# Attention's value products with the values stationary, two heads on the two column halves

## The reference

```python
def causal_block_attention(q, k, v):
    B, S, H, Dq = q.shape
    nb = S // Q_BLOCK
    scale = Dq ** -0.5
    qb = q.reshape(B, nb, Q_BLOCK, H, Dq).transpose(1, 0, 2, 3, 4)
    kpos = jnp.arange(S)

    def one_block(args):
        qi, idx = args
        s = jnp.einsum('blhd,bshd->bhls', qi, k, preferred_element_type=jnp.float32) * scale
        qpos = idx * Q_BLOCK + jnp.arange(Q_BLOCK)
        s = jnp.where(kpos[None, :] <= qpos[:, None], s, -jnp.inf)
        p = jax.nn.softmax(s, axis=-1).astype(v.dtype)
        return jnp.einsum('bhls,bshd->blhd', p, v)
...
    q = (rms_norm(c_q, q_gain) @ w_uq).reshape(B, S, A_HEADS, A_QK_DIM)
    kv = (rms_norm(c_kv, kv_gain) @ w_ukv).reshape(B, S, A_HEADS, A_NOPE + A_V_DIM)
...
    o = causal_block_attention(q, k, v)
```

## Time and profile before

| | |
|---|---|
| median of 3 runs | 1856.79 us |
| lowest, highest | 1854.67, 1859.2 us |
| span of the profiled execution | 1858.9 us |
| PE busy | 1745.5 us (94%) |
| DVE, ACT, POOL busy | 733.7, 424.0, 345.4 us |
| mean granted clock of TensorE | 0.974 |

### The profile page before, as it was taken

How to read it: one execution, slowest core, us unless ns; L and a number is a source line. 1 busy time by engine, 2 the same in 40 slices (tenths; PEclk the granted TensorE clock), 3 DMA queues, 4 the chain that set the end, 5 groups by cost and what they waited for, 6 DMA issues and landing times.

```text
span 1858.9 us, 25203 instructions
## 1 busy us (share of the span) xinstructions
PE 1745.5 (94%) x9534; PEld 1034.3 (56%) x9534; DVE 733.7 (39%) x1955; ACT 424.0 (23%) x1143; POOL 345.4 (19%) x381
## 2 busy tenths in 40 slices
PE   9999998888899999989799887999999999999998
PEld 5566555544446556655554443645668555466764
DVE  1844526421113462534721111334565233356533
ACT  3433321011112332322011111121332112123221
POOL 1100320332221010131133221000242000014300
PEclk9999989998999999989899998999999999999999
DMA  6121035899998111007599999612033121201401
GB/s 243 39 95 46 1 159 226 341 422 416 377 385 348 57 68 71 40 1 294 217 370 381 383 392 397 250 58 78 35 82 120 37 102 46 91 35 47 154 2 45
DMA packets 72535, 322.88 MB, mean 174 GB/s; under 512 B 26348, under 2 KB 40236, under 8 KB 50912
## 3 DMA queue, kind: packets, MB, share of 16 engines
q1 hardware_dynamic: 61536, 304.46, 41.8%
q0 software_dynamic: 10880, 16.82, 2.6%
HBM read 401.68 MB, written 28.85 MB: 232 GB/s over the span
## 4 chain that ended last, share of the span: by engine, by line
PE 80%; DMA 9%; DVE 6%; issue 3%; ACT 2%; SPq 1%; POOL 0%; POOLq 0%; DVEq 0%; ACTq 0%
PE bank L642 16%; PE bank L2444 10%; PE bank L1022 10%; PE bank L2430 8%; DMA b_arena<-in_w 7%; PE bank L1042 5%; PE bank L654 4%; PE bank L2619 3%; PE bank L2610 3%; PE bank L626 3%; PE bank L1007 1%; PE bank L2413 1%; PE bank L729 1%; PE bank L716 1%; PE bank L2405 1%
## 5 line engine op out<-in xcount | busy, mean ns | idle before, releaser
L642 PE MATMUL bank<-b_arena 128*128 128x512 f32 (+2 forms) x768 | 311.4, 558 | 5.3 <-DMA b_arena<-in_w_a 2.2
L1022 PE MATMUL bank<-b_arena,b_nat 128*32 128x256 f32 (+1 forms) x3008 | 258.7, 394 | 45.9 <-issue 27.9
L1022 PEld LDWEIGHTS bank<-b_arena,b_nat 128*32 128x32 f32 (+1 forms) x3008 | 156.5, 126 | 167.8 <-issue 80.4
L2444 PE MATMUL bank<-b_actT,b_ring 128*128 128x512 f32 x512 | 224.0, 594 | 0.0
L642 PEld LDWEIGHTS bank<-b_arena 128*128 128x128 f32 x768 | 144.5, 194 | 136.0 <-issue 105.1
L1500 DVE TENSOR_TENSOR b_nat<-bank,b_prm 128x512 f32<-128x512 f32 x68 | 47.0, 692 | 360.4 <-PE bank L1001 332.2
L2430 PE MATMUL bank<-b_ring,b_actT 128*128 128x384 f32 (+1 forms) x512 | 171.8, 492 | 3.0 <-DVE b_actT L3331 2.1
L2444 PEld LDWEIGHTS bank<-b_actT,b_ring 128*128 128x128 f32 x512 | 96.0, 190 | 114.9 <-issue 113.8
L1042 PE MATMUL bank<-b_arena,b_ebuf 128*32 128x512 f32 (+1 forms) x752 | 131.4, 601 | 19.1 <-ACT b_ebuf L1349 17.0
L2430 PEld LDWEIGHTS bank<-b_ring,b_actT 128*128 128x128 f32 x512 | 95.7, 190 | 70.4 <-issue 22.7
L1472 POOL DMA_INDIRECT y_rows<-b_va,b_rows_ix x68 | 69.6, 1023 | 343.5 <-ACT b_va L1357 334.7
(11 more groups left out here) (395 smaller groups left out, 2292.7 us busy)
## 6 DMA issues: line engine op xcount, KB each, us to landing
b_arena<-in_w SPq DMA_DIRECT2D x94, 2048.0 KB
b_arena<-in_w SPq DMA_DIRECT2D x94, 1024.0 KB
b_ring<-in_w_t SPq DMA_DIRECT2D x8, 2048.0 KB, 8.0
b_arena<-in_w SPq DMA_DIRECT2D x8, 1536.0 KB, 10.8
b_ring<-in_w_n2b SPq DMA_DIRECT2D x6, 1536.0 KB, 7.3
b_arena<-in_w_out SPq DMA_DIRECT2D x4, 2048.0 KB, 7.7
b_arena<-y_rows SPq DMA_DIRECT2D x16, 512.0 KB, 7.7
b_ring<-in_w_out SPq DMA_DIRECT2D x4, 2048.0 KB, 11.3
```

The source lines that it names most:

```text
L642: ins = pe.matmul(bank[:, 0:width], actT[:, k, tok(i)], w[:, k, :], start=k == 0, stop=k == KD - 1)
L1022: ins = pe.matmul(psum[2 + b % 2][f * CAP + at:f * CAP + end, 0:256], xgT[:, b % 2, k % 4, k // 4, at:end], w[half][:, k, f, :], start=k = ...
L2444: ins = pe.matmul(bank[:, :], w[:, k, tok(u % 4)], actT[:, k, :], start=k == 0, stop=k == KD - 1)
```

## The change

The roles of the operands are exchanged: the values (128x64) are loaded as the stationary operand and the transposed exponentials (128x128) stream past. The result is transposed: 64 value columns on partitions and 128 queries in the columns. Head 2p goes to partitions 0 to 63 and head 2p+1 to 64 to 127 of the same bank region. Since the rest of the kernel wants the queries on the partitions, ScalarE copies the result to SBUF (`oT`, in `w_uq`, which is free by then), PE transposes it back into a new bank (`on`, the same helper as for the exponentials), and VectorE copies it to `nat` as before. The work comes in ten groups a layer (`VALUES_AT`): tile 0 whole at u = 3; the pairs of heads of tile 1 at u = 4, 5, 6; those of tile 2 at 8, 10, 12; those of tile 3 at 14, 16, 18. `turn_values(g)` stands at the head of the next `attend`, the last one behind `out(0, 0)`. Twenty uses of banks take the place of 17, so most later uses have another bank and another predecessor than before. `a_squares` and `a_sums` of tiles 0, 1 and 2 move behind the next `attend`.

```diff
+VALUES_AT = [(3, 0, (0, 1, 2)), (4, 1, (0,)), (5, 1, (1,)), (6, 1, (2,))]
+VALUES_AT += [(8 + 6 * (i - 2) + 2 * p, i, (p,)) for i in (2, 3) for p in range(3)]
...
-        return [("sc", u)] * (u < UNITS) + [("pT", u - 1)] * (1 <= u <= UNITS) + [("av", u - 2)] * (u >= 2)
+        return ([("on", GROUP_AT.get(u - 1))] * (u - 1 in GROUP_AT) + [("sc", u)] * (u < UNITS)
+                + [("pT", u - 1)] * (1 <= u <= UNITS) + [("av", GROUP_AT.get(u))] * (u in GROUP_AT))
...
+            def turn_values(l, g):
+
+                _, _, ps = VALUES_AT[g]
+                pe.wait_ge(*emptied(l, "av", g))
+                transposed(l, "on", g, len(ps), lambda n: oT[:, g % 2, tok(n)])
+
             def attend(l, u):
 
+                if u - 1 in GROUP_AT:
+                    turn_values(l, GROUP_AT[u - 1])
...
-                if u >= 2:
-                    i, hs = UNIT[u - 2]
-                    pe.wait_ge(*emptied(l, "pT", u - 2))
-                    pe.wait_ge(*vacant(l, "av", u - 2))
-                    bank, full = writer(l, "av", u - 2)
-                    for n, h in enumerate(hs):
+                if u in GROUP_AT:
+                    g = GROUP_AT[u]
+                    _, i, ps = VALUES_AT[g]
+                    for t in sorted({unit_of(i, 2 * p + a) for p in ps for a in range(2)}):
+                        pe.wait_ge(*emptied(l, "pT", t))
+                    pe.wait_ge(*vacant(l, "av", g))
+                    bank, full = writer(l, "av", g)
+                    for n, p in enumerate(ps):
                         for j in range(i + 1):
-                            ins = pe.matmul(bank[:, n * AV:(n + 1) * AV], probT[:, u % 2, tok(n * (i + 1) + j)],
-                                            va[:, j, h, :], start=j == 0, stop=j == i)
+                            for a in range(2):
+                                t = unit_of(i, 2 * p + a)
+                                at = (2 * p + a - UNIT[t][1][0]) * (i + 1) + j
+                                ins = pe.matmul(bank[a * AV:(a + 1) * AV, tok(n)], va[:, j, 2 * p + a, :],
+                                                probT[:, t % 2, tok(at)], start=j == 0, stop=j == i)
...
                 out(l, 0, 0)
+                turn_values(l, VALUES - 1)
...
                     if u >= 3:
-                        act.wait_ge(*filled(l, "av", u - 3))
+                        act.wait_ge(*filled(l, "av", GROUP_OF[u - 3]))
                     copy_out(l, "pT", probT[:, (u - 1) % 2, 0:len(hs) * (i + 1) * P], u - 1)
+                if u in GROUP_AT:
+                    g = GROUP_AT[u]
+                    if g >= 2:
+                        act.wait_ge(*filled(l, "on", g - 2))
+                    copy_out(l, "av", oT[:, g % 2, 0:len(VALUES_AT[g][2]) * P], g)
...
-                attend(l, 18)
                 halves(l, "yT", 0, PC["mix"])
+                values_out(l, VALUES - 1)
```

More of the change, by code:

```diff
@@ L33, with unit_of @@
 UNITS = len(UNIT)
+VALUES_AT = [(3, 0, (0, 1, 2)), (4, 1, (0,)), (5, 1, (1,)), (6, 1, (2,))]
+VALUES_AT += [(8 + 6 * (i - 2) + 2 * p, i, (p,)) for i in (2, 3) for p in range(3)]
+VALUES = len(VALUES_AT)
+GROUP_AT = {v: g for g, (v, _, _) in enumerate(VALUES_AT)}
+def unit_of(i, h):
+    return next(u for u, (tile, hs) in enumerate(UNIT) if tile == i and h in hs)
+GROUP_OF = [next(g for g, (_, tile, pairs) in enumerate(VALUES_AT) if tile == i and hs[0] // 2 in pairs)
+            for i, hs in UNIT]
+assert all(VALUES_AT[GROUP_OF[u]][0] <= u + 3 for u in range(UNITS))
 M_AT = [0, S, 2 * S - P, 3 * S - 3 * P]
@@ L224, in order_one @@
     use += attend(14) + [("c", 2), ("csg", 0)] + attend(15) + [("csg", 1), ("c", 3)] + attend(16) + attend(17)
-    use += pair("yT", 0) + attend(18) + [("wo", 0), ("csg", 2), ("wo", 1)] + pair("yT", 1) + [("csg", 3), ("wo", 2)]
+    use += pair("yT", 0) + attend(18) + [("wo", 0), ("on", VALUES - 1), ("csg", 2), ("wo", 1)] + pair("yT", 1) + [("csg", 3), ("wo", 2)]
     use += pair("yT", 2) + [("wo", 3)] + pair("fT", 0) + [("wo", 4)] + pair("fT", 1) + [("route", 0)] + pair("yT", 3)
@@ L432, in block_one @@
         nat_flat = nat[:, :, :].rearrange("p t d -> p (t d)")
+        spare = w_uq[:, :, :].rearrange("p k n -> p (k n)")
         xg = [nat_flat[:, 512 * r:512 * (r + 1)] for r in (0, 1, 2, 3, 6, 7)]
@@ L1289, in run_scalar @@
                 attend(l, 3)
-                a_squares(l, 0, 0)
                 v_rows(l, 3)
                 attend(l, 4)
+                a_squares(l, 0, 0)
                 o_rows(l, 0)
@@ L1297, in run_scalar @@
                 attend(l, 6)
-                a_squares(l, 1, 1)
                 o_rows(l, 2)
                 attend(l, 7)
+                a_squares(l, 1, 1)
                 o_rows(l, 3)
@@ L1314, in run_scalar @@
                 m_decays(l, 3)
+                attend(l, 13)
                 a_squares(l, 4, 2)
-                attend(l, 13)
                 gelu_square(l, 1)
@@ L1331, in run_scalar @@
                 halves(l, "yT", 0, PC["mix"])
+                attend(l, 18)
                 c_squares(l, 9, 2)
@@ L1651, in attend, with values_out @@
                         ALU.mult).then_inc(*did("a_max"))
[L1652 to L1660 removed]
+                if u - 1 in GROUP_AT:
+                    values_out(l, GROUP_AT[u - 1])
+            def values_out(l, g):
+                _, i, ps = VALUES_AT[g]
+                dve.wait_ge(*filled(l, "on", g))
+                bank, free = reader(l, "on", g)
+                at, width = MW + ps[0] * P, len(ps) * P
+                dve.tensor_copy(nat[:, i, at:at + width], bank[:, 0:width]).then_inc(*free)
+                if ps[-1] == AH // 2 - 1:
+                    dve.wait_ge(*emptied(l, "on", g))
+                    dve.engine_nop().then_inc(*did("u_tile"))
             def m_weights(l, h):
@@ L1911, in run_vector @@
                 attend(l, 3)
+                attend(l, 4)
                 a_sums(l, 0, 0)
-                attend(l, 4)
                 keys_out(l, 3)
@@ L1916, in run_vector @@
                 attend(l, 6)
+                attend(l, 7)
                 a_sums(l, 1, 1)
-                attend(l, 7)
                 attend(l, 8)
```

13 lines of the change are left out of this document (2 added, 11 removed).

## The result

The changed kernel takes 1845.26 us (median of 4 executions, 1843.4 to 1849.92) where the kernel before takes 1856.15 (4 executions, 1854.67 to 1859.2): a ratio of 0.9935, 95% interval [0.992, 0.9951]. The forecast was 1850.9 with a range down to 1847: the sign is right, the size is not.

The account below looks back on a forecast made before the run. PE, busy 94% of the span, bounds the kernel, most tightly in attention. Full stretches 2.5 - short stretch 0.28 + tail 0.83 - transpose 0.11 = 2.94 us a layer, 5.9 for two: 1850.9 us, range 1847 to 1858.

Parts of the forecast that it names:

- Full stretches: Two stretches of each layer's attention where PE is always busy: 9.45 - 4.1 - 1.1 - 1.75 = 2.5 us less a layer.
- the way there and back: Switching PE to column halves and back: 0.25 us each time, seven groups a layer, 1.75 us more.
- 90 x 0.105 goes, 38 x 0.108 comes: Value products in the full stretches, a layer: 90 old records (9.45 us) replaced by 38 pairs of passes (4.1 us).
- Short stretch: 187.0 to 193.4 us, where PE waits for `gelu_out(0)`: group 6's ScalarE copy goes between, +0.28 us a layer.
- tail: End of attention, a chain through VectorE and ScalarE: `out(0,0)` starts 0.83 us sooner a layer.
- The wait of `m_scores(3)`: Sign in the short stretch: PE's wait there grows from 1.12 to about 1.4 us.
- The transpose in the tail: New transpose heading attend(17) starts near 233.3, delays the next transposes by 0.8 us, hidden; costs 0.8 if not.
- Rivals 1 and 2: 1: loads don't hide, pair 0.16 us, 1856.4 us, chance 0.15. 2: halves take turns, pair 0.216, 1862.6 us, chance 0.10.
- Rival 3, the clock: PE's longer pause in the tail delays clock recovery in `out(0,0)`: +1.3 to +4 us, 1852 to 1855, chance 0.09.
- free switches: Case where going to column halves and back costs nothing, giving 1847.4 us, the lower end of the forecast's own range.

Follow-up runs that it names:

- halves_apart: Changed kernel with the two loops exchanged, so PE gets all products of one head before those of the other: 1849.61 us, ratio 0.996.
- after_oldbanks: Changed kernel with the experts' PSUM banks laid out as in the kernel before: ratio 0.9936.
- before_warm: Kernel before, with idle products (8, 4 and 5) filling three pauses of PE in attention's tail: 1850.46 us, ratio 0.9968.
- after_pad: Changed kernel with 12 idle products a layer directly ahead of the new groups in the full stretches: 1852.14 us, ratio 0.9973.
- before_newbanks: Kernel before, with only the experts' PSUM banks laid out as in the changed kernel: ratio 0.9999.

## Why the prediction was right, and where it was wrong

**Full stretches: right.** Forecast -2.5 us a layer, measured -1.40 - 1.31 = -2.71. A pair costs the 0.108 us taken from the experts' products. Start to start, groups of six and eight products take 0.81 and 1.02 us where 0.65 and 0.87 were forecast: 0.15 to 0.16 more each, whatever the size. With the 0.09 that four transposes ahead of them take more, the way there and back costs 0.25, as forecast; it only shows inside the group instead of as a gap. That the fixed 0.16 is the price of going to the halves and back is a reading: the runs show that it doesn't grow with the group, not what it is. What the forecast did not see is that its own sum mixes two things. "90 x 0.105 goes, 38 x 0.108 comes" takes 14 records away altogether, 1.47 us, and these are moved, not made cheaper.

**Short stretch and tail: right.** +0.17 for +0.28; -0.82 for -0.83. The wait of `m_scores(3)` is 1.10 us and not 1.4: more value products stand in front of it. The transpose in the tail waits until 228.87, and nothing waits for it that counts, as forecast.

**Rivals 1 and 2: fallen.** Loads in series would have made eight records 0.64 us of work and 16 records 1.28; the difference between them is 0.43, not 0.64. The Trainium skill (TensorE: Matmul & The Clock Gate, Part 3, The mechanism) says that a weight load overlaps matmuls in flight only when its row group differs. Here both halves use all rows, and a pair takes 0.108 us where loads in series would make it 0.16: this case's trace doesn't agree. Halves taking turns would have made a pair 0.216 us; they don't while they alternate, and in halves_apart they do beyond some four records of each half.

**Rival 3, the clock: this is the step that failed.** The sum has no term for `out(0,0)` itself: it moves its start and adds the transpose behind it. The only word on its length is rival 3, which said that PE's pause in the tail gets longer, so that the clock might recover later, priced that at +1.3 to +4 us, and gave 9 in 100 to it; that it could recover sooner had no price at all. The direction was the wrong one. That `out(0,0)` took 10.03 us in one layer and 8.73 in the other, against 7.08 warm, was the sign that it can move either way, and that up to 4 us of gain lay there. By the table `out(0,0)`, with the new transpose behind it, takes 7.3 to 7.5 us in layer 0 instead of 9.86, and 8.1 to 8.6 instead of 8.57 in layer 1: 2.3 to 2.8 us over both in the three executions of the changed kernel, 1.7 in after_oldbanks. before_warm shows by itself that such time comes off the end.

What in the tail brings the clock back sooner is not settled. The change closes a pause of 1.09 us directly ahead of `out(0,0)` and puts 16 records where eight stood, and layer 0 gains; but layer 1 has the same tail and the same closed pause and gains 0.5 us at most. The grouping with the old operands closes the pause too: 8.16 us in layer 0, and in layer 1 8.70, no gain. Kernels with the same tail differ as well: after_pad has 8.44 in layer 0. So this part of the gain may turn out otherwise in another kernel with the same tail.

**The rest is not settled.** Attention and tail give 6.7 us, `out(0,0)` about 2.5; measured are 11.9. The remaining 2 to 3 us are about as large as the measurement's uncertainty. With the 6.7 and 2.5 us alone the forecast would have been about 1847.6, still above the 1845.26 measured, so the clock's term explains only part of the miss and the cause of the rest stays open. Over the table the measured gain is larger than the sum of segments in ten rows of twelve, by 1.7 us in the mean of all, so that something outside these segments may differ too; before_newbanks, with the same attention, speaks against a slip in the one profile of the kernel before. The other place where time differs is the experts' stage. It takes from 239.4 to 245.1 us in executions of one and the same changed kernel, in which PE's work is identical, and the kernel before has 244.45 and 245.34, both in the upper part (244.48 and 242.50 in before_newbanks). Whether its stages are longer on the whole would need many more profiled executions of it.

**The range.** Its lower end was the forecast with free switches, 1847.4, as if the terms were all that could vary. Executions of one kernel spread over 7 us or more here (the changed one from 1841.0 to 1849.9), and a median of a few moves by 1 to 2. The clock's term on the good side and that spread would have made the lower end about 1844.

## What to carry to other kernels

Where results are narrow (64 columns) and weights wide, exchanging the operands and putting two of them side by side takes half the time for each further product (0.108 us for two records instead of 0.105 for one), but count the transposes back and the way into and out of the halves: here, by the forecast's terms, 3.9 us a layer in the full stretches (76 x 0.105 - 4.1) became 1.05. Look too at where the products stand: moving 14 records out of the full stretches brought 1.49 there. And if a chain of waits stands ahead of a large group of products, price what the clock does in that group in both directions; idle products in the pauses ahead of it tested it in one run, and by themselves brought 5.9 us (3.2 by the segments), about half as much as the whole change.

## What the runs showed of the hardware that was not expected

- Products on two column halves overlap for about four records even if they are not alternated: 0.59 us for eight records either way; then each record of a longer run costs 0.11 to 0.12 us, as if alone, and sixteen take 1.52 us against 1.02. The Trainium skill (TensorEngine Tiling (Array Packing), Key Properties) says that tiles execute independently and in parallel; that holds here for alternating products, and only for the first records of long runs on one half.
- At the low clock the old form (128-column weights, 64 columns streaming) takes 3.65 us for 16 records and the new one 1.98.
- In the experts' stage, with the DMA engines busy 97% of it in layer 0, 14.6 us more of PE's work over both layers made the kernel only some 5 us slower. In before_newbanks PE's waits for late copies go from 7.5 and 9.4 us in the two layers to 1.0 each, and the kernel's time is the same (ratio 0.9999).
